# Up projections of a SwiGLU layer as seven half-size products per group, with GpSimd forming low parts of the gated activations

## The reference

```python
def swiglu(h, w_gate_up, w_down):
    gate, up = jnp.split(h @ w_gate_up, 2, axis=-1)
    return (jax.nn.silu(gate) * up) @ w_down
...
D_FF = -(-8 * D_MODEL // (3 * 256)) * 256          # 2816
        h = h + swiglu(rms_norm(h, ffn_norm[layer]), ffn_w_gate_up[layer], ffn_w_down[layer])
```

## Time and profile before

| | us |
|---|---|
| median of 3 runs | 1323.74 (1323.49 to 1324.98) |
| span of the profiled execution | 1322.1 |
| PE busy | 1313.7 (99%) |
| PEld busy | 1083.0 (82%) |
| DVE busy | 742.2 (56%) |
| ACT busy | 357.7 (27%) |
| POOL busy | 320.2 (24%) |

### The profile page before, as it was taken

The page is one execution under the profiler, slowest core; times in us unless marked ns, Lnnn a source line. Parts: engine busy times, 40 slices in busy tenths (PEclk is TensorE's granted clock), DMA queues, the critical chain, the costliest instruction groups (busy, mean ns, idle before and its releaser), DMA issues.

```text
span 1322.1 us, 17282 instructions
## 1 busy us (share of the span) xinstructions
PE 1313.7 (99%) x6414; PEld 1083.0 (82%) x6414; DVE 742.2 (56%) x1084; ACT 357.7 (27%) x730; POOL 320.2 (24%) x358
## 2 busy tenths in 40 slices
PE   9999999999999999999999999999999999999998
PEld 8888778888888888888888878888888888888886
DVE  8987856456774443344435778466764443334432
ACT  5247455124521110001112347335421110001112
POOL 2222145213311111112111136324212111111110
...
GB/s 228 105 103 112 94 74 81 81 96 95 117 93 101 100 99 96 96 96 96 95 96 112 108 113 55 65 96 97 95 96 96 95 96 96 96 96 97 100 89 96
DMA packets 97681, 130.38 MB, mean 99 GB/s; under 512 B 6320, under 2 KB 62896, under 8 KB 97616
## 3 DMA queue, kind: packets, MB, share of 16 engines
...
...
## 4 chain that ended last, share of the span: by engine, by line
PE 92%; DVE 5%; issue 1%; DMA 0%; ACT 0%; SPq 0%; POOL 0%; DVEq 0%; POOLq 0%; ACTq 0%
PE ps L643 25%; PE ps L647 25%; PE ps L646 25%; DVE xc L1455 1%; PE ps L1204 1%; PE ps L1205 1%; PE ps L1201 1%; PE ps L1034 1%; DVE w_lo L1233 1%; PE ps L1050 1%; PE ps L1063 1%; PE ps L923 1%; PE ps L954 1%; PE ps L846 1%; PE ps L941 1%
## 5 line engine op out<-in xcount | busy, mean ns | idle before, releaser
L1233 DVE TENSOR_TENSOR w_lo<-raw,w_hi 128x1024 fp32r<-128x1024 f32 x225 | 278.6, 1240 | 413.2 <-POOL w_hi L574 411.2
L574 POOL TENSOR_SCALAR w_hi<-raw 128x1024 fp32r<-128x1024 f32 x226 | 248.1, 1098 | 902.0 <-DMA raw<-in_w_gate_up 403.6
L643 PE MATMUL ps<-z_hi,w_hi 128*128 128x512 f32 x1040 | 406.8, 391 | 0.3 <-DVE z_lo L1253 0.2
L647 PE MATMUL ps<-z_hi,w_lo 128*128 128x512 f32 x1040 | 404.9, 389 | 0.0
L646 PE MATMUL ps<-z_lo,w_hi 128*128 128x512 f32 x1040 | 404.8, 389 | 0.0
L643 PEld LDWEIGHTS ps<-z_hi,w_hi 128*128 128x128 f32 x1040 | 195.2, 188 | 46.3 <-issue 5.0
L647 PEld LDWEIGHTS ps<-z_hi,w_lo 128*128 128x128 f32 x1040 | 195.2, 188 | 41.0
L646 PEld LDWEIGHTS ps<-z_lo,w_hi 128*128 128x128 f32 x1040 | 195.3, 188 | 40.0
L643 PE MATMUL ps<-f_hi,w_hi 128*128 128x512 f32 x528 | 206.4, 391 | 0.6 <-DVE w_lo L1233 0.4
L647 PE MATMUL ps<-f_hi,w_lo 128*128 128x512 f32 x528 | 205.6, 389 | 0.0
L646 PE MATMUL ps<-f_lo,w_hi 128*128 128x512 f32 x528 | 205.5, 389 | 0.0
...
## 6 DMA issues: line engine op xcount, KB each, us to landing
...
```

What stands on the lines that cost most here:

```text
L574: pool.tensor_scalar(w_hi[:, slot], raw[:, slot], 1.0, 1.0, ALU.mult, ALU.mult).then_inc(s_hi, 1)
L643: ins = pe.matmul(o, whi, rhi, start=start, stop=False)
L647: return pe.matmul(o, wlo, rhi, start=False, stop=stop)
L1233: dve.tensor_tensor(w_lo[:, slot], raw[:, slot], w_hi[:, slot].bitcast(F32), ALU.subtract).then_inc(s_lo, 1)
```

## The change

Of the 11 pairs of feature tiles of a layer, the first three (`PLAIN`) are projected as before. Each of the other eight becomes two "quads", one for gate and one for up: a product of 256 features, 1024 inputs and 512 tokens, cut in half along each of the three, and formed in seven half-size products (kinds 1 to 7) in place of eight. A half-size product is 128 features by 512 inputs by 256 tokens: 4 tiles by 3 matmuls, 12 matmuls of 256 columns, so a quad has 84. Before, two tiles of gate or of up were 48 matmuls of 512 columns. There are 6 quads in the first chunk of a layer and 10 in the second.

The activations are brought to `rstd` scale, halved and summed into seven operands once per layer (`z_scaled`, `z_sum`, `z_low` on DVE, `z_high` on ACT) during the plain groups. Per quad, DVE forms four sums of weight blocks (`weight_sum`, 128x512 each) and seven low parts (`weight_low`), ACT forms the seven high parts (`weight_high`), and POOL makes no high parts there. The products are accumulated in three PSUM banks in the order 5, 2, 6, 3, 7, (1 of the next quad), 4; between them ACT copies intermediate sums to SBUF (`copy`: c1, c5, u2, u3, 128x256 each), and a later product that adds to the same bank waits for the copy. DVE adds up the quarters from banks and copies (L2100, L2110, L2115; from here on lines are those of the changed kernel). The low part of the gated activations of the quads (`f_low`, two 128x512 subtractions per pair of quads) is moved from DVE to POOL. Loops in this part are written out.

The core of the diff:

```diff
+PLAIN = 3
+QUADS = (CHUNK[0] - 2 * PLAIN, CHUNK[1])
...
+KIND_SLOT = {1: 0, 5: 1, 2: 2, 6: 3, 3: 4, 7: 5, 4: 6}
...
+DONE = counts((1,), ((0, 5), (0, 2), (0, 6), (0, 3), (0, 7), (1, 1), (0, 4)))
...
+        AFTER_RUN = {UNIT0[f"down{l}{c}"] + j: (QUAD0[l, c] + QUADS[c], j) for l, c in runs() for j in range(SLOTS)}
...
+                for n in range(QUADS[c]):
+                    q = QUAD0[l, c] + n
+                    col = f0 + 256 * (n // 2 + (0 if c else PLAIN)) + D_FF * (n % 2)
+                    for half in range(2):
+                        slot = 2 * (n % 2) + half
+                        if n < 2:
+                            slot_left(sp, l, c, slot)
+                        elif half == 0:
+                            sp.wait_ge(s_p, DONE[q - 2, 1])
+                            sp.wait_ge(s_v, SUMMED[q - 2, 3])
+                        else:
+                            sp.wait_ge(s_p, DONE[q - 2, 3])
+                        src = w_gate_up[l][4 * P * half:4 * P * (half + 1), col:col + 256]
+                        sp.dma_start(quad_raw[:, slot], src.rearrange("(a p) n -> p a n", p=P)).then_inc(s_qraw[slot], 32)
                 stream(f"down{l}{c}", w_down[l][f0:f0 + CHUNK[c] * P, :], CHUNK[c] // 2)
...
+            def f_low(l, c):
+                for n in range(1, QUADS[c], 2):
+                    r, tile = (QUAD0[l, c] + n) // 2, 2 * (PAIRS0[l, c] - 11 * l - sum(CHUNK[:c]) // 2 + n // 2)
+                    if n == 1 and c == 0:
+                        pool.wait_ge(s_ff_lo, 2 * PAIRS0[l, c])
+                    for p, hi in ((1, 1), (0, 3)):
+                        pool.wait_ge(s_q_hi, 3 * r + hi)
+                        pool.tensor_tensor(f_lo[:, tile + p, :], ff_u[:, p, :], f_hi[:, tile + p, :].bitcast(F32),
+                                           ALU.subtract).then_inc(s_ff_lo, 1)
...
+                for c in range(2):
+                    high(at_unit, UNIT0[f"down{l}{c}"])
+                    f_low(l, c)
+                    at_unit = UNIT0[f"down{l}{c}"]
...
+            def quad_product(l, q, i, o, start):
+                first_of_layer = q == QUAD0[l, 0]
+                if first_of_layer:
+                    pe.wait_ge(s_zql, 7 * l + Z_LOWS.index(i) + 1)
+                pe.wait_ge(s_wl, LOW[q, i])
+                for k in range(4):
+                    whi, wlo = kind_hi(i)[:, k, :], kind_lo(q, i)[:, k, :]
+                    zh, zl = zq_hi[:, i - 1, k, :], zq_lo[:, Z_SLOT[i], k, :]
+                    pe.matmul(o, whi, zh, start=start and k == 0, stop=False, skip_group_check=True)
+                    pe.matmul(o, whi, zl, start=False, stop=False, skip_group_check=True)
+                    ins = pe.matmul(o, wlo, zh, start=False, stop=k == 3, skip_group_check=True)
...
+                first_product(0)
+                for n in range(n_quads):
+                    q = QUAD0[l, c] + n
+                    a, b, d = home(n, 0), home(n, 1), home(n, 2)
+                    quad_product(l, q, 5, d, True)
+                    quad_product(l, q, 2, b, True)
+                    pe.wait_ge(s_cp, COPIED[q, "c1"])
+                    quad_product(l, q, 6, a, False)
+                    pe.wait_ge(s_cp, COPIED[q, "c5"])
+                    quad_product(l, q, 3, d, False)
+                    pe.wait_ge(s_cp, COPIED[q, "u2"])
+                    quad_product(l, q, 7, a, False)
+                    if n + 1 < n_quads:
+                        first_product(n + 1)
+                    pe.wait_ge(s_cp, COPIED[q, "u3"])
+                    quad_product(l, q, 4, a, False)
...
                 attention(ax, l, lambda j, tiles=range(MB): memory_values(l, j, tiles), ahead(*xo))
                 stage(*xo, first=1)
+                stage(f"up{l}0", 4, zf, s_ff, ready=z_ready(f"ffn{l}"), norm=f"ffn{l}")
                 for c in range(2):
-                    stage(f"up{l}{c}", 4, z, s_ff, ready=z_ready(f"ffn{l}") if c == 0 else None,
-                          norm=f"ffn{l}" if c == 0 else None)
+                    quads(l, c)
...
+                def weight_sum(q, i):
+                    if q >= 2:
+                        dve.wait_ge(s_p, DONE[q - 2, (5, 6, 7, 4)[i - 1]])
...
+                    dve.tensor_tensor(quad_v[:, q % 2, i - 1], x, y, ALU.subtract).then_inc(s_v, 1)
...
+                def weight_low(q, i):
+                    dve.wait_ge(s_wh, HIGH[q, i])
+                    dve.tensor_tensor(kind_lo(q, i), kind_full(q, i), kind_hi(i).bitcast(F32), ALU.subtract).then_inc(s_wl, 1)
...
+                    def product_h1(n):
+                        r = (QUAD0[l, c] + n) // 2
+                        dve.wait_ge(s_q_silu, 3 * r + 3)
+                        dve.wait_ge(s_p, DONE[QUAD0[l, c] + n, 4])
+                        dve.tensor_tensor(ff_u[:, 0, QHALF:], ff_g[:, 0, QHALF:], home(n, 0), ALU.mult).then_inc(s_q_prod, 1)
...
+                    for n in range(n_quads):
+                        q, up, more = QUAD0[l, c] + n, n % 2, n + 1 < n_quads
+                        ff = ff_u if up else ff_g
+                        if n and not up:
+                            product_h1(n - 1)
+                        weight_low(q, 6)
+                        if more:
+                            weight_sum(q + 1, 1)
+                            weight_low(q + 1, 1)
+                        weight_low(q, 3)
+                        if n:
+                            free(n - 1)
+                        if n == 0:
+                            rest()
+                        if up and n > 1:
+                            dve.wait_ge(s_ff_lo, 2 * (PAIRS0[l, c] + n // 2))
+                        dve.wait_ge(s_p, DONE[q, 2])
+                        dve.wait_ge(s_cp, COPIED[q, "c1"])
+                        dve.tensor_tensor(ff[:, 0, 0:QHALF], home(n, 1), copied["c1"][:], ALU.add).then_inc(s_c, 1)
+                        if more:
+                            weight_sum(q + 1, 2)
+                        weight_low(q, 7)
+                        if more:
+                            weight_sum(q + 1, 4)
+                            weight_sum(q + 1, 3)
+                        weight_low(q, 4)
+                        dve.wait_ge(s_p, DONE[q, 3])
+                        dve.wait_ge(s_cp, COPIED[q, "u2"])
+                        dve.tensor_tensor(ff[:, 1, 0:QHALF], home(n, 2), copied["u2"][:], ALU.add).then_inc(s_c, 1)
+                        if more:
+                            weight_low(q + 1, 5)
+                            weight_low(q + 1, 2)
+                        dve.wait_ge(s_cp, COPIED[q, "u3"])
+                        dve.tensor_tensor(ff[:, 1, QHALF:], copied["u3"][:], copied["c5"][:], ALU.add).then_inc(s_c, 1)
+                        if up:
+                            r = q // 2
+                            dve.wait_ge(s_c, 3 * q + 3)
+                            dve.wait_ge(s_q_silu, 3 * r + 2)
+                            dve.tensor_tensor(ff_u[:, 1, :], ff_g[:, 1, :], ff_u[:, 1, :], ALU.mult).then_inc(s_q_prod, 1)
+                            dve.tensor_tensor(ff_u[:, 0, 0:QHALF], ff_g[:, 0, 0:QHALF], ff_u[:, 0, 0:QHALF],
+                                              ALU.mult).then_inc(s_q_prod, 1)
+                    product_h1(n_quads - 1)
+                    free(n_quads - 1)
+                    low_to(down0 + 2)
+                plain_gate(0)
+                low_to(up0 + 7)
+                plain_up(0)
...
+                quad_begin(QUAD0[l, 0])
+                def rest_of_plain():
+                    plain_gate(2)
+                    plain_up(2)
+                    plain_product(2)
+                    plain_low(2)
+                quads(0, rest_of_plain)
+                down0 = UNIT0[f"down{l}0"]
+                residual("mix1", f"down{l}0", group0=GROUP0[f"down{l}0"], norm_next=False,
+                         units=(down0 + CHUNK[0] // 2, down0 + CHUNK[0]), between=lambda: quad_begin(QUAD0[l, 1]))
+                quads(1, lambda: None)
...
+                def weight_high(c, n, i):
+                    q = QUAD0[l, c] + n
+                    if n:
+                        act.wait_ge(s_p, DONE[q - 1, i])
+                    else:
+                        slot_left(act, l, c, KIND_SLOT[i] // 2)
+                    if i in (1, 2, 3):
+                        slot = 2 * (q % 2) + (0 if i == 1 else 1)
+                        act.wait_ge(s_qraw[slot], 32 * (q // 2 + 1))
+                    else:
+                        act.wait_ge(s_v, SUMMED[q, {5: 1, 6: 2, 7: 3, 4: 4}[i]])
+                    act.activation(kind_hi(i), kind_full(q, i), ACT.Copy).then_inc(s_wh, 1)
...
+                    copy(0, "c1", 1, 0, 1)
+                    for n in range(n_quads):
+                        q, up, more = QUAD0[l, c] + n, n % 2, n + 1 < n_quads
+                        if up:
+                            act.wait_ge(s_p, DONE[q - 1, 4])
+                            silu(q - 1, home(n - 1, 0), 2)
+                        weight_high(c, n, 3)
```

(32 more changed lines are left out.)

421 lines of the change are left out of this document (303 added, 118 removed).

## The result

| | before | after |
|---|---|---|
| median, us | 1324.24 (4 runs, 1323.49 to 1324.98) | 1351.14 (4 runs, 1350.83 to 1351.58) |
| span of the profiled execution, us | 1322.1 | 1349.0 |
| PE busy, us | 1313.7 | 1305.4 |
| PE idle, us | 8.4 | 43.6 |

The changed kernel is slower: ratio 1.0203, 95% interval 1.0189 to 1.0218, or 26.9 us. The forecast was 1332 us, a loss of 8.6; the range ended at 1348. The direction was right; the forecast loss is a third of the measured one.

The account below looks back on a forecast made before the run. PE was taken to bound the kernel. 1322.1 - 25.6 (products) + 1 (inside quads) + 17.0 (run ends) + 9.4 (first quads) + 6.8 (clock) = 1330.7 us of span, 1332 as median; range 1320 to 1348.

Parts of the forecast that it names:

- seven products: In each quad, 84 matmuls at 0.120 us replace 48 at 0.2267; over 32 quads 25.6 us less.
- four run ends: PE waits before the down stage for a chain through DVE, ACT, POOL and DVE: 4.67 us each, 17.0 in all.
- first quads: In each layer's first quad, product 7 waits for copy u2 behind the third plain group's evacuation: 4.7 us, twice, 9.4.
- inside the quads: Waits of PE in the quads' steady state, from POOL running beside DVE: 1 us, bounds 0 and 16.
- clock: PE's clock falls to 1.2 GHz in the long gaps, 1.25 us lost per gap of 4.7: 6.8 us in all.
- The pace of 0.120: In the quads, 256-column matmuls start 0.120 us apart, 12 in 1.44 us.
- rival E: Quad matmuls pace at 0.109 us, by the skill page's rule, instead of 0.120: 29.6 us less, 1303; 5%.
- B: Same gaps at the seams, but the clock holds at 2.4 GHz: 1325.5 us; 14%.
- A sign of being wrong: PE idle before products inside later quads would show the forecast wrong, and was tied to DVE as the bound.
- D: DVE becomes the bound inside the quads, by whole durations, contention and in-order waits: up to 16 us, 1347; 16%.
- I take 1, by the slack: In the quads, DVE's loss beside POOL, up to 1.6 us per pair, is mostly covered by 1.3 to 3.8 of slack.
- rival C: At run ends POOL starts `w_hi` before product 4 ends, so gaps are 2.1 us: median 1318; 9%.

Follow-up runs that it names:

- experiments one: Changed kernel with POOL's high parts and DVE's low parts of the first two down units ordered earlier at run ends: 1325.02 us, 1.0005.
- nine: Changed kernel with one added wait: POOL's second `w_hi` at a run's end starts only after DVE's first `w_lo`: 1346.47 us, 1.0167.
- experiment three: Changed kernel with the third plain group's evacuation split on DVE and ACT in each layer's first quad: 1341.82 us, 1.0133.
- experiment five: Changed kernel with POOL's `f_lo` covering 8 columns instead of 512, except in each run's last pair: 1344.15 us, 1.0146.
- experiment four: Changed kernel with unread extra matmuls filling PE's gaps, 40 per run end and 28 before product 7 in each layer's first quad: 1341.22 us, 1.0129.
- experiment two: Changed kernel with only POOL's high part of the first down unit moved ahead of the last pair's low parts: 1335.51 us, 1.0086.
- Experiment ten: Changed kernel with run-end reordering, split evacuation, POOL's `f_lo` held back and first `w_lo` ahead of the last quad's u3 quarter: 1303.55 us, 0.9842.

## Why the prediction was wrong

| term, us | forecast | read or measured |
|---|---|---|
| seven products | -25.6 | -25.6, by the pace |
| four run ends | +17.0 | +22.3; experiments one, nine |
| first quads | +9.4 | +8.1; experiment three |
| inside the quads | +1 | +9.3: 6.8 by POOL beside DVE (experiment five: 7.0), 2.5 by copy u3 (read from the trace; no experiment removed it) |
| clock | +6.8 | +9.9; experiment four |
| ahead of the quads | 0 | +1.8 in the profiled execution, mostly scatter |
| sum | +8.6 | +25.8 of 26.9 |

**Where it was right.** The pace of 0.120 (rival E falls), both seams, the chain at each and the engine that releases it, and that the clock falls (B falls). The first quads were forecast 1.3 us too dear, 0.6 each: copy u2 ended 11.2 us after the start of product 1 and not 11.7, and PE went on 0.06 us later and not 0.22. A sign of being wrong that the prediction named did appear, idle time before products inside later quads; it named it for D, and half of D was behind it, the contention and the waits in order, but not a DVE that is short of time.

The formula behind rival E needs a word. On its page (the Trainium skill, TensorE: Matmul & The Clock Gate, Back-to-back issue gap) it is the gap of an isolated matmul; for a stream of matmuls with weight loads the page has about 131 ns at 512 columns. The trace agrees with neither: 227 ns.

**"I take 1, by the slack"** is the step that failed most: the term for waits inside the quads was 1 us, and they cost 9.3. The rows gave a warning: a DVE instruction beside POOL took 0.8 us longer. Two things went wrong with them. The loss was set against DVE's slack over a whole pair of quads (1.3 to 3.8 us), but slack can't be carried there: at the beginning of an even quad, low part 6, two instructions for the next quad and low part 3 stand in a row behind the last product, and product 3 waits for their end. Both `f_lo` fall beside just that row: the first starts when ACT has the high part of the tile that is complete early (617.29), the second behind that of the last product (618.94). And the forecast used one loss of up to 0.8, where an instruction that starts just behind `f_lo` lost 1.1 (1.79 against 0.68). The place was named ("a few tenths might show"), but a few tenths were not multiplied by the 12 times that it comes round: 12 x 0.57 was inside the bound of 16 that the prediction kept. The other 2.5 us are a plain omission. It had worked out that one product covers copy u3, and did not ask what covers it in a run's last quad, where there is no next product 1.

**The run end was 1.35 us too short** (4.67 against 6.02), by two links. One `f_lo` was counted, but there are two, and the first can't start before ACT's high parts, so POOL is busy until 504.98: 0.19 by the duration (1.24 against the 1.05 taken, inside its bounds) and some 0.4 by the queue. And `w_lo` was taken alone at 1.22, though POOL's next instruction is another `w_hi` that starts with it: 0.8, which experiment nine confirms. The bounds of 4.3 to 5.0 held neither, since they varied a duration and not the structure.

The Trainium skill (GPSIMD Engine Reference, Elementwise) has 4497 ns for 2048 columns; a quarter is an estimate of 1.1 us. The trace has 1.24 alone and 1.30 to 1.35 beside DVE.

**The clock** term was 3.1 us short: 6.8 against 9.9. The prediction took one row, a fall 2.5 us after PE's last work, both for when a fall comes and for how long PE then works slowly. The fall came 2.2 to 5.2 us after PE's last matmul, the slow work was 3.2 to 4.2 us per gap and not 2.5, and the gap of the last run, which the sum gave half a chance and 0.5 us, had 3.4 us of it. Nor is 2.5 us a limit below which a gap is safe or above which it is not, as rival C's sum had it: an idle time of 2.64 us met a fall at two places of three, and one of 3.26 us met none.

**Rival C** was wrong in its condition: POOL did not start `w_hi` before product 4 had ended. Made true in experiment two, its gap was 2.80 and not 2.1, again by contention (`w_lo` 1.84 beside `f_lo`), and the clock fell in it twice.

Open: 1.1 us of the 26.9, of which 0.4 stand right behind the waits for u3, since the product there takes 0.09 longer each time. Experiment ten has a span 5.5 us above 1322.1 - 25.6 = 1296.5: 2.5 are the u3 waits, 1.2 lie ahead of the up projections (its 2001st matmul starts at 399.57), and the rest is in small waits that were not followed up.
